# Order of the first transfers, an engine for the first remainder, and the place of the first tile in a two-block network kernel

## What is computed

```python
sh, sc, g = jnp.split(sc_lat @ w_ada[i] + b_ada[i], 3, axis=-1)
h  = rmsnorm(x,  norm_g[i]) * (1.0 + sc[:, None, :]) + sh[:, None, :]
shc, scc, gc = jnp.split(sc_ctx @ w_ada[i] + b_ada[i], 3, axis=-1)
hc = rmsnorm(xc, norm_g[i]) * (1.0 + scc) + shc
# in mlstm_inputs, for both h and hc:
xm, o_pre, z = jnp.split(hmod @ w_in, 3, axis=-1)
```

## Time and profile before

| what | value |
|---|---|
| median of 3 runs | 1219.07 us (1217.16 to 1220.79) |
| the profiled execution's own time | 1220.43 us |
| its span | 1218.6 us |
| TensorE busy | 1180.9 us (97%) |
| VectorE, ScalarE, GpSimd busy | 860.9, 615.5, 147.0 us |
| mean granted TensorE clock | 0.992 of full speed |

### The profile page before, as it was taken

One profiled execution on the slowest core, in us unless ns is written; L12 is line 12 of the kernel. 1 busy time (PEld: TensorE's weight loads), 2 busy tenths in 40 slices (PEclk: granted clock), 3 DMA queues, 4 the chain that ended last, 5 costly groups with the idle time before them and its releaser, 6 DMA issues.

```text
span 1218.6 us, 22951 instructions
## 1 busy us (share of the span) xinstructions
PE 1180.9 (97%) x9274; PEld 1099.8 (90%) x9274; DVE 860.9 (71%) x1443; ACT 615.5 (51%) x1003; POOL 147.0 (12%) x115
## 2 busy tenths in 40 slices
PE   6999999999999999999999899999989999999996
PEld 3777898988888999999999899999989998999995
DVE  4795885468789767666498787674579967866644
ACT  4432655466664455662453544453466765445433
POOL 0000000000000000003001323210007830222000
PEclk8999999999999999999999999999999999999998
DMA  9856412233222356442544455555433233545540
GB/s 387 329 216 245 170 70 70 104 132 138 94 94 106 137 185 237 164 147 70 188 173 159 146 182 192 179 197 177 173 114 131 103 121 123 201 179 178 201 175 35
DMA packets 28900, 195.59 MB, mean 160 GB/s; under 512 B 3464, under 2 KB 3728, under 8 KB 6416
## 3 DMA queue, kind: packets, MB, share of 16 engines
q1 hardware_dynamic: 27776, 191.90, 43.5%
q10 hardware_dynamic: 1040, 2.50, 0.6%
HBM read 193.33 MB, written 1.05 MB: 160 GB/s over the span
## 4 chain that ended last, share of the span: by engine, by line
PE 88%; DVE 4%; ACT 3%; DMA 3%; POOL 1%; issue 1%; SPq 0%; ACTq 0%; DVEq 0%; POOLq 0%
PE ps L489 26%; PE ps L490 25%; PE ps L491 25%; PE ps L842 2%; PE ps L516 1%; DMA ada_room<-in_weights 1%; PE ps L534 1%; PE ps L829 1%; PE ps L662 1%; DMA ring<-in_weights 1%; DVE w_lo L1773 1%; ACT x_hi L1462 1%; PE ps L1070 1%; PE ps L721 1%; PE ps L888 1%
## 5 line engine op out<-in xcount | busy, mean ns | idle before, releaser
L1156 ACT ACTIVATE w_hi<-ring 128x1024 fp32r<-128x1024 f32 x284 | 294.6, 1054 | 289.3 <-PE ps L491 202.9
L1773 DVE TENSOR_TENSOR w_lo<-ring,w_hi 128x1024 fp32r<-128x1024 f32 x266 | 327.6, 1251 | 151.3 <-ACT w_hi L1156 144.7
L489 PE MATMUL ps<-x_hi,w_hi 128*128 128x258 f32 (+1 forms) x1216 | 346.6, 285 | 7.6 <-DVE x_lo L2153 4.1
L490 PE MATMUL ps<-x_lo,w_hi 128*128 128x258 f32 (+1 forms) x1216 | 344.2, 283 | 0.0
L491 PE MATMUL ps<-x_hi,w_lo 128*128 128x258 f32 (+1 forms) x1216 | 343.8, 283 | 0.0
L489 PEld LDWEIGHTS ps<-x_hi,w_hi 128*128 128x128 f32 x1216 | 231.0, 190 | 11.6 <-issue 11.4
L490 PEld LDWEIGHTS ps<-x_lo,w_hi 128*128 128x128 f32 x1216 | 231.3, 190 | 0.1
L491 PEld LDWEIGHTS ps<-x_hi,w_lo 128*128 128x128 f32 x1216 | 230.9, 190 | 0.0
L489 PE MATMUL ps<-g_hi,w_hi 128*128 128x256 f32 x608 | 171.1, 281 | 3.6 <-ACT logit L1583 1.5
L490 PE MATMUL ps<-g_lo,w_hi 128*128 128x256 f32 x608 | 170.2, 280 | 0.0
L491 PE MATMUL ps<-g_hi,w_lo 128*128 128x256 f32 x608 | 170.2, 280 | 0.0
(11 more groups left out here) (378 smaller groups left out, 1936.9 us busy)
## 6 DMA issues: line engine op xcount, KB each, us to landing
ring<-in_weights SPq DMA_DIRECT2D x148, 1024.0 KB, 4.8
o_sb<-in_weights SPq DMA_DIRECT2D x10, 1024.0 KB, 7.2
ada_room<-in_weights SPq DMA_DIRECT2D x10, 1024.0 KB, 8.5
ring<-in_weights SPq DMA_DIRECT2D x8, 512.0 KB, 4.1
ring<-in_weights SPq DMA_DIRECT2D x8, 448.0 KB
V<-in_weights SPq DMA_DIRECT2D x3, 1024.0 KB, 24.3
dft<-in_dft ACTq DMA_DIRECT2D x1, 1026.0 KB, 7.3
X<-in_x SPq DMA_DIRECT2D x1, 1024.0 KB, 5.0
```

Source lines behind the costliest of these rows:

```text
L489: mm(dst, w_h, x_h, start=start, stop=False, skip_group_check=True)
L490: mm(dst, w_h, x_l, start=False, stop=False, skip_group_check=True)
L1156: do(w_hi[:, q % 2, part], ring[:, q % RING, part], ACT.Copy).then_inc(S("hi_ready"), 1)
L1773: v.tensor_tensor(w_lo[:, q % 2, part], ring[:, q % RING, part], w_hi[:, q % 2, part], ALU.subtract).then_inc(S("lo_ready"), 1)
```

## The change

The first slot's weights are loaded behind the first two modulation blocks. ScalarE's first rounding moves behind the move of the first pair. The first half's remainder is formed by GpSimd instead of VectorE, and VectorE waits before each later remainder for the one before. TensorE's first tile stands ahead of the fourth modulation block.

```diff
             sp.dma_start(ctx_room, ctx_in).then_inc(S("ctx_ready"), 16)
-            load(0)
             for a in range(N_ADA0):
                 load_ada(a)
+                if a == 1:
+                    load(0)
                 if a == 3:
                     load(1)
@@ TensorE
             pair_turn(0)
             ada_rows(2)
+            first_tile(0, 0)
             ada_rows(3)
-            first_tile(0, 0)
             first_tile(0, 1)
@@ ScalarE
             do(V[:, HC, :], ps[:, 7, :], ACT.Copy).then_inc(S("sums_moved"), 1)
-            rounded_half(0, 0)
             act.wait_ge(S("meansq_0"), 1)
...
                 do(V[:, p, 0:SEQ], ps[:, PAIR_BANKS[p % 2], 0:SEQ], ACT.Copy).then_inc(S("ada_moved"), 1)
-                if p:
-                    rounded_half((1, 0, 1)[p - 1], p // 2)
+                rounded_half(p % 2, p // 2)
@@ GpSimd
+            pool.wait_ge(S("hi_ready"), 1)
+            pair_op(w_lo[:, 0, 0:SLOT // 2], ring[:, 0, 0:SLOT // 2], w_hi[:, 0, 0:SLOT // 2], ALU.subtract)\
+                .then_inc(S("lo_ready"), 1)
             pool.wait_ge(S("scores_done"), HEADS)
@@ VectorE
-            rest_of_half(0)
             dve.wait_ge(S("root_0"), 1)
...
                 if p:
+                    dve.wait_ge(S("lo_ready"), p)
                     rest_of_half(p)
```

## The result

The changed kernel takes 1222.61 us (median of 20 runs, 1220.65 to 1227.37) against 1219.87 us for the kernel before (20 runs in the same comparison, 1217.16 to 1224.0). The ratio is 1.0023, 95% interval [1.0015, 1.003]: 2.7 us slower, between 1.8 and 3.7. The forecast was 1220.2, 1.1 us slower and leaning to slower, with a range to 1223.2. Direction and range hold; the size is more than twice what I worked out. A profile shows one execution: that of the changed kernel took 1223.77 us, 1.2 us more than its median, and that of the kernel before 1220.43 us, 0.6 us more than its own.

What follows compares the result with a forecast made beforehand. TensorE, busy 97% of the span, bounds the kernel, so shifts at the beginning reach the end. VectorE's first group +0.95 us, then ada_rows(3) and the second remainder behind the tile, give +1.1: 1219.07 + 1.1 = 1220.2 us, range 1216.9 to 1223.2.

Steps and rivals of the forecast that it cites:

- These land at 11.5 and 14.0: Opening transfers: two modulation blocks trade places with the first weights, landing at 11.5 and 14.0 instead of 13.98 and 16.46.
- the exclusion: First modulation: GpSimd's remainder blocks VectorE's two-SBUF-operand scl from 17.95 to 19.98; VectorE's first group moves by +0.95 us.
- a tile that was to fill the gap lengthens it: TensorE's beginning: the first tile starts at 22.55, ahead of ada_rows(3), lengthening the gap of 20.0 to 21.43.
- P: Theory in the follow-ups: the tile's place is the price; ada_rows(3), landed at 21.4, waits behind a tile whose h completes at 22.3.
- the mark: Start of first_tile(1, 0), 28.54 us before; behind it the order is the same in both kernels; forecast to move to 29.65.
- +1.1: Forecast shift in us of first_tile(1, 0)'s start, from 28.54 to 29.65, added to the kernel's time.
- ada_rows(0) and (1), both landed, run from 13.5 to 15.5: TensorE's first two passes: they run from 13.5 to 15.5; before, the second started at 16.46, 2.0 us earlier now.
- case A: The forecast itself: GpSimd holds VectorE up, +1.1 us; the clock spreads it from -0.1 to +2.0; chance 0.55.
- one for one: Whatever is won or lost before TensorE's unbroken work, or in a stall shortly after, reaches the kernel's end in full.
- C: Rival at the first remainder: VectorE's unbroken work keeps GpSimd out, +3.0 to +3.5 us, slower; chance 0.12.
- D: Rival at the first remainder: GpSimd's first use costs extra, +3.1 us, or +4.6 by the skill's estimate; chance 0.06.
- B: Rival: no exclusion, the tile fills the gap, -0.9 us, 1218.2; 1215.1 with the clock kept at 2.4 GHz; chance 0.22.

Runs made afterwards that it cites:

- e4: The changed kernel with GpSimd's first remainder formed for only 64 of 1024 columns, the rest left at zero: 1220.32 us, ratio 1.0006 to the kernel before.
- e6: The changed kernel again, unchanged, for a second profile: 1222.98 us in one run, against 1219.84 for the kernel before.
- e9: The changed kernel with the first two slots loaded in halves, tile order back, first rounding ahead of the first pair's move: 1218.17 us, ratio 0.999 to before.
- e1: The changed kernel with the first tile back behind the fourth modulation block: 1219.69 us, ratio 0.9999 to the kernel before.
- e3: The kernel before with only the tile order changed, first tile ahead of the fourth modulation block: 1220.86 us, ratio 1.0011 to the kernel before.
- e11: The changed kernel again, unchanged, for a third profile: 1221.93 us, ratio 1.0027 to the kernel before.
- e2: The changed kernel with the first remainder formed by VectorE, ahead of the first modulation, instead of GpSimd: 1220.92 us, ratio 1.0009 to the kernel before.
- e12: The half-load version of e9 again, for a second sample and profile: 1218.64 us, ratio 0.9992 to the kernel before.
- e8: The changed kernel with four extra unused matmuls where TensorE waits in the beginning: 1220.75 us, ratio 1.0005 to the kernel before.
- e10: The half-load version of e9 with two extra unused matmuls where TensorE waits for transfers: 1218.89 us, ratio 0.9991 to the kernel before.
- e7: The kernel before with two extra unused matmuls where TensorE waits for transfers: 1221.67 us, ratio 1.0011 to the kernel before.

## Why the prediction held, and where its size failed

*Transfers.* "These land at 11.5 and 14.0": confirmed by the passes from 13.50 on, with no wait between them, and by ScalarE's rounding at 16.36 (16.46 forecast).

*RECIPROCAL and the exclusion.* RECIPROCAL from 14.33 (14.42), GpSimd 17.50 to 19.85 (17.6 to 19.98), scl to 19.87 (20.12), the tile at 22.39 (22.55). e4 shows the cause by taking it away. The Trainium skill's rule (SBUF — State Buffer, "Who interferes with whom") was applied to an operation of 4 columns and holds: 2.13 us in the first profile, 2.36 in e6, 0.16 in e4. The prediction calls the section silent on RECIPROCAL, but this section of the Trainium skill says that a VectorE instruction with at most one input in SBUF, outside the two-port modes, doesn't contend with GpSimd. RECIPROCAL lasted 3.35 us as before (3.34), in the first profile with only 0.2 us of it beside GpSimd, in e9 with 1.5.

*The order of TensorE.* The step "a tile that was to fill the gap lengthens it" holds: e1 takes it away and the loss with it; e3 adds it alone and has about half of it. The tile was ready at 22.3 for a gap that closed at 21.3. So P is the cause, and it needs both parts: with the order undone (e1) or GpSimd's hold gone (e4) the interval of the time ends below that of the changed kernel. At the mark it is +1.39 against +1.1 forecast.

*A step that held in only two profiles of three is "ada_rows(0) and (1), both landed, run from 13.5 to 15.5".* I took these passes at 2.4 GHz as the profile of before had them, and saw the clock's chance only behind 20 us (case A's -0.1 to +2.0). They did run from 13.50 to 15.43 in the first profile and in e11, but in e6 they lasted 3.06 us, and in e2 3.64. With their blocks early they aren't paced by transfers any more, and ScalarE's rounding and with it GpSimd's start stand behind them: 1.3 us later in e6, the tile at 23.68.

*The term that was mis-sized is the clock's.* +1.1 was worked out; at the mark the changed kernel's three profiles (29.93, 29.96 and 30.50) are 1.4, 1.4 and 2.0 us behind the 28.54 of before, and 0.2 more behind its second profile's 28.31. The medians say 2.7 and 2.8. The prediction carried the mark's lag "one for one" to the end, and two things stand between. At 136 us 0.4, 1.1 and 0.0 us are caught up. Then low stretches of the clock, for which the sum has no term, cost 1.5 and 0.8 us in the first profile, 0.6 in e6 and nothing more in e11. The prediction named the clock at later gaps only for a time outside its range. That the measured time lies inside is in part luck: the range reached so far up by what C and D would cost, and by the spread of the runs.

Do such stretches belong to the change? Three profiles can't tell: e3 and e9 had the longer one near 890 too, and e4, e9 and e12 the one near 690. But the record has the mean granted clock of every execution. It is 0.9901 on average over the changed kernel's 29 executions and 0.9917 over 100 of the kernel before; it is 0.990 or less in 22 of the 29 and in 29 of the 100. A us at the low level takes half a us from that share, so the changed kernel spends about 3.9 us more there (twice 0.0016 of 1220 us). With the tile's order undone (e1) the average is 0.9919 over 11 executions, with GpSimd's hold gone (e4) 0.9918 over 12: the extra comes and goes with the loss. Some of it lies in the beginning, where the profiles of the changed kernel have 10.2, 6.8 and 10.2 us at the low level and those of before 6.8 and 6.8. How the rest is shared between 690, 890 and 1010 us, and by what way a shift of 1 to 2 us in the beginning brings it about, stays open.

The Trainium skill (TensorE: Matmul & The Clock Gate, "Part 1: The HAM clock gate") says that where the clock changes varies from run to run of one kernel. The profiles agree: the first low stretch behind 12 us begins at 20.8, 20.5 (before), 17.5, 13.2, 17.6 (changed).

*The rivals.* B fell for this kernel, by the 2.13 us of scl, and came true in e4 at the tile and the mark, though not in the time (1220.32 us, where B has 1218.2). C and D fell: GpSimd's operation began 0.1 us ahead of modl in the first profile and level with scl in e6, and won both times; it lasted 2.35 us, its first use included. The Trainium skill (GPSIMD Engine Reference, "Instruction dispatch") gives about 6 us for the first call into a freshly loaded kernel; the estimate of +4.6 us from it falls too, for no such time stands ahead of this operation or in it.

## What to carry to other kernels

Before giving work to GpSimd, look at which two-operand operations VectorE runs in that stretch: an operation of four columns can wait for the whole of GpSimd's. Before filling a gap of TensorE with a ready piece, compare when the piece is ready with when the gap ends, and count what stands behind it in the queue. A lag read at the start isn't yet the time at the end: match the two traces further down. And when a transfer is moved away from in front of an engine, what was paced by the transfer becomes paced by the clock: price it at both levels.

## What the runs showed beyond that

Small amounts of unused work went with a clock at 2.4 GHz through a beginning with many gaps: in e8 and e10 the first low stretch came only at 891 and 887 us, while every other profile had one that began between 12.7 and 22.3 us. In e7 it lay at 12.7 to 16.2, and the first extra matmul stands behind ada_rows(0), which ran to 16.1. One profile each could be chance, but the mean granted clock over 12 executions each is 0.9928, 0.9932 and 0.9934 in e7, e8 and e10, against 0.9917 before and 0.9901 in the changed kernel.

The transfers of half slots had a price. The 8 us from 12 to 20 in the changed kernel and in e10 (the last number is GB/s, the one before it the DMA engines' busy share):

```profile
12.00:20.00 8.00, 4.70 (x50) 2.35 (x54) 5.96 (x6) 2.52 (x4) 2.35 (x1) 0.84 1.01 422
```

```profile
12.00:20.00 8.00, 5.95 (x57) 2.69 (x58) 5.91 (x7) 2.81 (x5) 2.35 (x1) 1.00 0.99 389
```

All of the loss lies between 12 and 16 us, while the first half slot travels: 371 and 350 GB/s in the two windows of 2 us in e9, 360 and 348 in e10, 375 and 354 in e12, against 418 and 426 in the changed kernel, with the engines as busy. That is worth about 0.6 us, the 0.6 us by which modulation 3 came later than a strict share of the bytes would give. From 16 us on the rate is about 420 GB/s again on average, though the second slot's first half travels there too (it lands near 21.9 in e9), so why the rate falls stays open.
